# Seven products of quarter matrices for the up projection of a two-layer decoder step

## The reference

```
x = x + rmsnorm(mix, nm_post)
hf = jnp.einsum('btd,df->btf', rmsnorm(x, nf_pre), w_up)      # 1024 -> 4096
f = jnp.einsum('btf,fd->btd', jnp.square(jax.nn.relu(hf)), w_down)   # 4096 -> 1024
x = x + rmsnorm(f, nf_post)
```

## Time and profile before

| | |
|---|---|
| median of 3 runs | 2558.09 us (2558.03 to 2558.55) |
| profiled execution | 2556.82 us, of which the span of the trace is 2555.0 us |
| TensorE (PE) busy | 2509.7 us (98%) |
| VectorE (DVE) busy | 1397.3 us (55%) |
| ScalarE (ACT) busy | 795.3 us (31%) |
| GpSimd (POOL) busy | 963.2 us (38%) |
| mean granted TensorE clock | 0.998 |
| mean DMA rate | 73 GB/s |

### The profile page before, as it was taken

How to read it: one execution, slowest core, us unless ns; L and a number is a source line. 1 busy time by engine, 2 the same in 40 slices (tenths; PEclk the granted TensorE clock), 3 DMA queues, 4 the chain that set the end, 5 groups by cost and what they waited for, 6 DMA issues and landing times.

```text
span 2555.0 us, 45179 instructions
## 1 busy us (share of the span) xinstructions
PE 2509.7 (98%) x17828; PEld 2264.7 (89%) x17828; DVE 1397.3 (55%) x1966; ACT 795.3 (31%) x1281; POOL 963.2 (38%) x443
## 2 busy tenths in 40 slices
PE   8999999999999999999999999999999999999998
PEld 6996666988999999999989866669899999999998
DVE  5546666358346445643664566662684455345526
ACT  3125555234112111211441255551431112112214
POOL 2431000215664565455214300003065655664541
PEclk9999999999999999999999999999999999999999
DMA  6114332221111011010331153323211110111013
GB/s 229 44 38 127 90 88 83 110 83 60 67 50 47 35 52 63 22 61 33 135 118 42 40 135 89 87 67 118 85 51 66 50 66 16 66 49 57 25 42 144
DMA packets 99962, 187.12 MB, mean 73 GB/s; under 512 B 30704, under 2 KB 43184, under 8 KB 99824
## 3 DMA queue, kind: packets, MB, share of 16 engines
q1 hardware_dynamic: 97120, 176.83, 21.2%
q0 software_dynamic: 2560, 8.39, 1.2%
q10 hardware_dynamic: 144, 0.00, 0.0%
HBM read 158.85 MB, written 23.11 MB: 71 GB/s over the span
## 4 chain that ended last, share of the span: by engine, by line
PE 81%; issue 7%; DVE 5%; ACT 3%; POOLq 2%; POOL 1%; DVEq 1%; SPq 1%; DMA 0%; ACTq 0%
PE psum L1991 37%; PE psum L2487 21%; PE psum L2181 3%; PE psum L1976 3%; PE psum L2207 3%; PE psum L2193 2%; PE psum L2084 2%; PE psum L2228 2%; PE psum L2021 1%; ACT z L1010 1%; DVE stat L1569 1%; PE psum L2514 1%; PE psum L2264 1%; PE psum L2241 1%; PE psum L2239 1%
## 5 line engine op out<-in xcount | busy, mean ns | idle before, releaser
L1991 PE MATMUL psum<-hh,wh 128*128 128x352 f32 x2064 | 668.8, 324 | 0.8 <-DVE z L1419 0.8
L1991 PE MATMUL psum<-hh,wl 128*128 128x352 f32 x2064 | 662.8, 321 | 0.0
L1991 PE MATMUL psum<-hl,wh 128*128 128x352 f32 x2064 | 662.7, 321 | 0.0
L685 POOL TENSOR_TENSOR wh<-raw,ones 128x1024 fp32r<-128x1024 f32 x106 | 205.4, 1937 | 539.8 <-PE psum L1991 429.1
L2487 PE MATMUL psum<-hidh,wh 128*128 128x264 f32 x1344 | 384.6, 286 | 7.3 <-issue 4.1
L1991 PEld LDWEIGHTS psum<-hh,wh 128*128 128x128 f32 x2064 | 387.9, 188 | 2.6 <-issue 1.7
L1991 PEld LDWEIGHTS psum<-hl,wh 128*128 128x128 f32 x2064 | 388.5, 188 | 0.8
L1991 PEld LDWEIGHTS psum<-hh,wl 128*128 128x128 f32 x2064 | 387.5, 188 | 0.0
L2487 PE MATMUL psum<-hidl,wh 128*128 128x264 f32 x1344 | 383.7, 285 | 0.0
L2487 PE MATMUL psum<-hidh,wl 128*128 128x264 f32 x1344 | 382.8, 285 | 0.0
L1779 DVE TENSOR_TENSOR z<-psum,z 128x528 f32<-128x528 f32 x360 | 246.0, 702 | 129.4 <-PE psum L2487 129.4
(11 more groups left out here) (286 smaller groups left out, 4231.8 us busy)
## 6 DMA issues: line engine op xcount, KB each, us to landing
raw<-wst SPq DMA_DIRECT2D x104, 512.0 KB, 3.4
z<-cache_c SPq DMA_DIRECT2D x352, 64.0 KB, 1.9
x<-x_spill SPq DMA_DIRECT2D x4, 4224.0 KB, 14.5
t<-wst SPq DMA_DIRECT2D x56, 256.0 KB, 4.0
raw<-cache_c SPq DMA_DIRECT2D x160, 64.0 KB, 1.9
x_spill<-x SPq DMA_DIRECT2D x2, 4224.0 KB, 13.8
x_spill<-x SPq DMA_DIRECT2D x6, 1408.0 KB, 5.2
cn<-wst SPq DMA_DIRECT2D x28, 256.0 KB, 3.3
```

What stands on the lines that cost most here:

```text
L685: pool.tensor_tensor(wh[:, s, :], src, ones[:, 0:1].to_broadcast([P, TW]), ALU.mult)
L1991: ins = pe.matmul(bank3(u, g), w[:, s, o:o + P], m[:, k, cols(g)], start=(k == 0 and n == 0), stop=(k == kk - 1 and n == 2))
```

## The change

The up projection of blocks 1 to 7 is done like the down projection: seven products (`UPS`) of 512 x 512 weight quarters with 512 x 528 input quarters. I call them f0 to f6. A product is two units of 24 matmuls over 264 tokens.

**Input quarters.** Four sums of input quarters (T_1 to T_4) and the quarter B_22 are made once per layer: x is loaded again from DRAM in quarters (into space of `x2` and `hl`), ACT scales it with the gains (`gained`), DVE and POOL subtract, ACT and DVE make high and low parts (`high_t`, `low_t`), and SP stores both parts in DRAM (`keep`). The two right-hand places of `hh` and `hl` hold by turns what each product needs; from block 2 on ACT issues five loads per block (`load`), two DMAs of 1.08 MB each.

**Weights.** All eight quarters of a block are loaded as quarters by SP (`weights_of`); POOL makes the four sums for the up projection too (`sum_1` to `sum_4`), ACT all high parts and POOL all low parts (`low_one`).

**Out of PSUM.** ACT copies the first results (`copies`), DVE adds the others (`added`), and relu is now a separate DVE instruction from SBUF to SBUF for three of the four quarters (`relu_of`, `last_relu`).

The diff, cut to what matters. The products, each with its slot of weights (2 is `cw`), its input quarter, its PSUM bank set, and whether it starts it fresh:

```diff
+UPS = [(2, 0, 1, 1, True), (0, 0, 0, 0, True), (1, 1, 1, 0, False), (0, 0, 1, 1, False),
+       (1, 1, 0, 1, True), (0, 1, 1, 0, False), (1, 0, 1, 0, False)]
```

SP, once per layer, from block 0's down projection on (`splits(n)` waits for the n-th pair of weight parts, counted from g1's):

```diff
+                splits(1)
+                quarter_in(u21, up1, 1, 0, up_q)
+                sp.wait_ge(hl_new.sem, at.whole(hl_new, KD))
+                keep(B_22, 1, hq3_out)
...
+                sp.wait_ge(hq3_out.sem, at.value(hq3_out))
+                sp.dma_start(part_of(hl_raw, 0, 1), part_of(xs, 0, 0)).then_inc(xa_in.sem, 16)
+                sp.dma_start(part_of(x2, 0, 1), part_of(xs, 0, 1)).then_inc(xa_in.sem, 16)
+                sp.dma_start(part_of(hl_raw, 1, 1), part_of(xs, 1, 1)).then_inc(xb_in.sem, 16)
+                sp.dma_start(part_of(x2, 1, 1), part_of(xs, 1, 0)).then_inc(xb_in.sem, 16)
...
+                sp.wait_ge(t_lo.sem, at.value(t_lo, 1))
+                keep(T_1, 0, hq1_out)
+                splits(6)
+                quarter_in(u12, up1, 0, 1, up_a12)
+                sp.wait_ge(tr_pool.sem, at.value(tr_pool, 1))
+                sp.dma_start(flat(tq[1]), part_of(x2, 1, 1)).then_inc(hq3_out.sem, 16)
...
+                sp.wait_ge(t_lo.sem, at.value(t_lo, 2))
+                keep(T_2, 1, hq3_out)
...
+                def weights_of(tile, again, first):
+
+                    quarter_in(a22, tile + 4, 1, 1, dn_q, 0)
+                    quarter_in(a21, tile + 4, 1, 0, dn_q)
+                    quarter_in(a11, tile + 4, 0, 0, dn_a11, 2)
+                    quarter_in(a12, tile + 4, 0, 1, dn_a12, 3)
...
+                    quarter_in(u22, tile + 8, 1, 1, up_q, 5)
...
+                    quarter_in(u21, again, 1, 0, up_q, 6)
```

POOL, one block; the twelve low parts (one in each of `low_one` and `last_sum`) are for f2 to f6, g1 to g6 and the next f1, in this order:

```diff
+                def block_parts():
+
+                    low_one(1, u21)
+                    sum_3(u21, u22)
+                    sum_1(a21, a22, dn_q, up_full, 2)
+                    low_one(0, us4)
+                    low_one(1, u12)
+                    sum_2(a21, a11, dn_a11)
+                    low_one(0, u21)
+                    sum_4(s4, a12, a21, dn_a12)
+                    low_one(1, u22)
...
+                    low_one(0, s4)
+                    low_one(1, a11)
+                    sum_1(u21, u22, up_q, dn_full, PH)
                     low_one(0, a21)
+                    sum_3(a21, a22)
                     low_one(1, a21)
                     low_one(0, a22)
+                    next_ups()
                     low_one(1, a12)
...
+                    last_sum()
```

ACT in block 0, and then ACT in a later block from the end of f6 on (`weight(n)` makes the high part for POOL's n-th low part):

```diff
                     high_sum(3, two, 0, b12)
+                    gained(hl_raw, 0, 1, 0, xa_in)
+                    gained(x2, 0, 1, 0, xa_in)
                     high_sum(1, both, PH, b11)
                     at.step(s2_new)
                     act.wait_ge(s2_new.sem, at.value(s2_new))
                     high_down(0, 3, a21)
...
+                    high_down(0, 7, u11)
...
+                    high_t(1, 0, hq3_out, 48)
...
+                    load(T_1, 0, hq1_in, 14)
...
+                    weight(7, a11)
+                    square_of(b21)
+                    high_sum(3, both, 0, b12)
+                    high_sum(1, both, PH, b11)
+                    new_sum(s2_new)
+                    weight(8, a21)
+                    high_sum(2, both, 2 * PH, b12)
+                    new_sum(s3_new)
+                    weight(9, a21)
```

DVE, down projection of blocks 1 to 6 (`low(1, both, b11)` is for g4, and ACT's part of it is `high_sum(1, both, PH, b11)`):

```diff
+                        ups_of()
+                        less(b12, b22, b12, both).then_inc(h_sum.sem, 1)
+                        take(0, TURN)
+                        low(0, both, b11)
+                        dve.drain()
+                        low(3, both, b12)
+                        take(1, TURN)
+                        less(b11, b12, b11, both).then_inc(h_sum.sem, 1)
+                        squares_done(1)
+                        less(b12, b21, b12, both).then_inc(h_sum.sem, 1)
+                        take(2, TURN)
+                        low(1, both, b11)
+                        take(3, TURN)
+                        low(2, both, b12)
```

More of the change, by code:

```diff
@@ L181, in build @@
             pass
+        with nc.sbuf_tensor("hl_raw", [P, KD, TOK], F32) as hl_raw:
+            pass
         hl = sb("hl", [P, KD, TOK], F32R)
@@ L223, in build @@
         s4 = raw[:, 0, :]
+        u11, u12, u21, u22, us4 = a21, a12, raw[:, 0, :], raw[:, 1, :], a11
         b11, b12 = z[:, 8:10, 0:HB], z[:, 8:10, HB:TOK]
@@ L1238, in _ @@
+                first_half(False)
+                last_hid(0, 1, b12)
+                weight(5, u22)
+                for row, half, part in ((0, 0, b11), (1, 1, b22), (1, 0, b21)):
+                    square_of(part)
+                    last_hid(row, half, part)
+                at.step(up_full, UH)
                 act.wait_ge(fsq_free.sem, at.value(fsq_free))
@@ L1854, in block_of @@
-                    low(3)
-                    for m in range(UNITS_DOWN if not last else 4):
-                        if last and m == 2 and l < DEPTH - 1:
+                    for u in range(2):
+                        added(3, 1, 0, 1, u)
+                    relu_of(b12, 1)
+                    for u in range(2):
+                        added(4, 1, 0, 0, u)
+                    relu_of(b11, 0)
+                    added(5, 0, 1, 1, 0)
+                    low(0, 1, b12)
+                    added(5, 0, 1, 1, 1)
@@ L1857, in block_of @@
+                    relu_of(b22, 1)
+                    low(0, 0, b11)
+                    last_relu(0)
+                    last_relu(1)
+                    at.step(up_full, UH)
+                    at.step(up_act, 6)
+                    low(1, 1, b22)
+                    low(1, 0, b21)
+                    for m in range(4):
+                        if m == 2 and l < DEPTH - 1:
                             at.step(pre_in, 16)
```

606 lines of the change are left out of this document (433 added, 173 removed).

## The result

| | before | after |
|---|---|---|
| median of the runs on the same chip | 2558.32 us (2558.03 to 2560.24) | 2659.09 us (2654.28 to 2660.23) |
| ratio, 95% interval | | 1.0389 (1.0371 to 1.0407) |
| profiled execution, its span | 2556.82, 2555.0 us | 2659.99, 2658.2 us |
| forecast | | 2617 us, range 2558 to 2650 |

What follows compares the result with a forecast made beforehand. PE, busy in 98% of the span, was taken to bound the kernel. The terms gave 2556.8 - 64.8 + 50 + 34 + 40 = 2616.0, the median 1.3 above: 2617 us, 2.3% slower, range 2558 to 2650.

Steps and rivals of the forecast that it cites:

- matmuls saved, 7 blocks: Up projection, 7 blocks of 2 layers: seven products take 41.17 us in place of 45.80, 4.63 less each, -64.8 us.
- stops, block 0: Block 0's down projection: g3 waits for x, then g4's weight and g5 are held; 17 us a layer, +34 (23 to 38).
- stops, block 1, both projections: Block 1: f2, f3 and later operands wait for stores and loads, 20 us a layer; its down projection loses 4.2.
- stops, blocks 2 to 6: Down projection of later blocks: g2, g3, g4 late, 4.2 us a block; +50 us over blocks 1 to 6, both layers.
- block 7's end: End of block 7: costed at nothing, since 24 matmuls of down_first cover the last relu; without it some 2 us.
- the rival: Clock falls in the long stalls at f3 and g3: 4 stops, 5.88 us more each, 2640 us; chance 0.06.
- the trace has no such stop to tell: Clock: granted 1.00 in every stretch read, longest feed-forward stop 2.09 us, so no case of PE's clock falling when idle.
- The walk: A whole later block followed with DVE and POOL meetings: g2 1.3 late, g3 1.9, g4 1.0, sum 4.2 us.
- The least case: Down projection of a later block: g3 at least 1.06 late, 2.15 us in all the least a block can lose.
- The prediction's three parts: Block 0's down projection: g3 13.7 us late, g4's weight held 1.9, g5 held 2.6; together called 17 a layer.
- f2 and f3 together: Block 1's up projection: both products wait for stores and loads, 15 to 20 us late together, or 10.
- loads become the bound: Later blocks' up projection: 4.8 MB at 277 GB/s, T_4 2.8 us late in 12 blocks, 2651 us; chance 0.11.

Runs made afterwards that it cites:

- the first experiment: Changed kernel with the vector engine's difference for g3's quarter moved ahead of two takes and a low part in blocks 1 to 7; 2655.98 us, 1.0388.
- the run with SyncE's order: Changed kernel with only SyncE's block 0 transfers reordered: a22 and a21 ahead of T_2's store, B_22's store ahead of u21; 2627.47 us, 1.0272.
- the two runs with a stop made in the kernel before: Kernel before the change, ScalarE repeating the copy for g3's weight in the loop's blocks: three extra copies 2594.88 us, five 2627.55 us.
- the last version: Changed kernel with new SyncE, ScalarE, vector and GpSimd orders and T_1 loaded later, finally GpSimd's differences behind f5's and f6's low parts; 2557.29 us, 0.9987.

## Why the prediction was right in its side and wrong in its size

For the first layer, from the windows above (stops: length less busy PE, less what the kernel before had; clock: busy PE above full clock):

| us per layer | forecast | measured |
|---|---|---|
| matmuls saved, 7 blocks | -32.4 | -33 (86.9 - 82.2 = 4.7 each) |
| stops, block 0 | 17 | 14.6 - 3.0 = 11.6 |
| stops, block 1, both projections | 20 + 4.2 | 25.4 - 0.1 = 25.3 |
| stops, blocks 2 to 6 | 5 x 4.2 = 21 | 19.3 - 0.5 = 18.8 |
| block 7's end | 0 | 1.0 |
| PE at the lower clock | 0 | 5.1 + 8.7 + 8.8 = 22.6 |
| later start of g0 (2.8 of it not by the change, see below) | 0 | 617.99 - 611.48 = 6.5 |
| sum | 29.8 | 52.8 |

**The step that failed** is the clock: the sum had nothing for it, and it stood beside the sum as a rival only. Its mechanism was right, but it was given 0.06, four places and 5.88 us each, 23 in all. The loss is 22.6 us in the first layer and, by the same windows of the second, 16.2, so 39 in both: without it the changed kernel would stand at 2659 - 39 = 2620, beside a forecast of 2617. Both factors were off. A place cost less than a whole product at half clock: 13 to 27 of the 48 matmuls ran so, for 1.4 to 2.8 us. And there were 20 places and not 4: the rival was applied to stops over 10 us only, while stops from 1.9 us on brought it too, seven of them in the middle blocks. And "the trace has no such stop to tell" was not true: I had read the clock in the first layer, where the stop of 2.09 us had none behind it. The same place in the second layer of the kernel before has the answer:

```profile
1897.40 0.56 PE L2487 MATMUL psum<-hidh,wh 128*128 128x264 f32 x1 [2.06 <-issue]
```

```profile
1897.40:1904.80 7.40, 7.39 (x48) 7.40 (x49) 5.05 (x7) 2.44 (x3) 4.18 (x2) 0.77 0.00 1
```

A stop of 2.06 us, then a product of 7.4 at a clock of 0.77.

That all the rest comes to within 3 us is in part luck. The stops of the first layer are 56.7 us where 62.2 were forecast, and the later g0, which had no term, put 6.5 in their place.

**Waits of the middle blocks:** 4.2 a block forecast, 3.8 measured. The walk put 1.3, 1.9 and 1.0 before g2, g3 and g4; in block 3 and most others it was 0.3, 3.4 and 0. DVE's sum met not one but two instructions of GpSimd, so g3 took the whole delay and g4 none. The sum of a walk held where its places did not; for the clock the places mattered, since one stop of 3.4 costs a slow product and three of 1 to 1.7 do not (the first experiment). The least case, 2.15, came out as 2.2 when GpSimd's sums were out of the way.

**Block 0:** g3 forecast at 646.1, measured at 646.47, by the steps named: ACT's `gained` started at 635.58 behind the DMA, 0.8 later than forecast. Behind it PE stood 0.9 around g4 in place of 1.9, and 2.6 before g5 as forecast, from start to start. (The prediction's three parts, 13.7, 1.9 and 2.6, make 18.2 and not the 17 that it went on with.) The stops are only 11.6 where 17 were forecast because g3's time was set by the DMA and by ACT, whenever g0 began: 6.5 us of its lateness came out as a later g0. **Block 1:** f2 2.6 to 3 forecast, 4.2 measured; f2 and f3 together 15 to 20, measured 17.5; GpSimd's wait for the quarter behind T_2's store was the cause, as the run with SyncE's order showed with its 31.6 us.

**The later start of g0** had no term. 3.7 of its 6.5 us were in the units before g0: more of GpSimd's first `sum_1` now runs beside DVE's `low_h`, which took 10.02 us for five instructions in place of 6.24 in the kernel before. The sum waits for two quarters in place of four, and begins 3.1 us behind the start of `low_h` in place of 5.4. I costed the change from f0 on only. First the kernel before, then the changed one:

```profile
590.09 6.24 DVE L1380 SCALAR_TENSOR_TENSOR hl<-x,gn,hh 128x1056 fp32r<-128x1056 f32 x5
```

```profile
592.89 10.02 DVE L1663 SCALAR_TENSOR_TENSOR hl<-x,gn,hh 128x1056 fp32r<-128x1056 f32 x5
```

The other 2.8 us had built up before the feed-forward part, and are not the change's: the two runs with a stop made in the kernel before, whose code is the kernel before's up to there, begin the same five instructions at 592.89 and 593.01. So single executions differ by that much ahead of the part, and the first layer's loss by the change is some 50 us.

**Loads.** The rival "loads become the bound" is settled for the middle blocks: 182 GB/s at trips of 82.93 us, with no wait for them. In block 1 it was right in kind: f3's stop of 3.5 to 7.7 us in the first layer of the versions with SyncE's new order is ended by a load of B_22 (1.6 us where T_2's store was held back). ACT's share was also somewhat higher than taken: 0.53 and 0.65 us per DMA where I had 0.43.

**The middle blocks' cause** is shown to be order, not amount: in the last version the same 25 instructions of GpSimd take 61 us of 83, and the stops are gone. With GpSimd's order alone changed, g3's stop had fallen from 3.4 to 1.1. A trip fell by 87.82 - 82.93 = 4.9 us in the first layer and by 4.3 in the second. What remains is in blocks 0 and 1. Counted from the start of block 0's up projection, block 0 takes 9.5 us more than before the change in the first layer of the last version (670.05 - 592.85 for 655.95 - 588.26) and 8.2 in the second, and block 1 takes 11.3 and 11.6 more (98.37 and 98.66 for 87.03 and 87.05). That eats the gain of the matmuls. Whether it can be had back was not shown: splitting block 1's sum or taking its weights first left f3's stop, and holding back T_2's store moved it to f4.

## What to carry to other kernels

On a queue that makes small things with near due times (the low part of each weight) and large ones with far due times (the sum for the next stage), write down for each when it is wanted, and put the large ones in pieces behind the small ones; a place that looks free is only as free as the next due time behind it. When a stop of PE is moved or split, look at the clock behind it as well as at its length. And before you write that a trace has no case of something, look in every layer.

## What the runs showed of the hardware

I counted, over the feed-forward parts of all 18 traces, each stop of PE (distance of two matmuls' starts less 0.12 us) and whether the granted clock fell to 0.5 in the 48 matmuls behind it, or up to the next stop; there the matmuls follow each other at 0.22 us in place of 0.12:

| stop | stops | with half clock behind |
|---|---|---|
| 0.9 to 1.85 us | 316 | 0 |
| 1.85 to 2.2 us | 65 | 26 |
| 2.2 to 3.4 us | 82 | 60 |
| over 3.4 us | 129 | 125 |

At half clock PE runs at 1.2 GHz; the loss behind a stop was 1.4 to 2.8 us in the changed kernel. Behind the shorter stops the clock often fell only some matmuls into the product, up to 12, so a look at the first few misses it. The same stop, at the same place of the same loop, brings it or not, which is why the middle blocks of one kernel differ (86.93 to 88.87 us). The Trainium skill ("TensorE: Matmul & The Clock Gate", Part 1: The HAM clock gate) says that TensorE is throttled when idle and gets its clock back by activity, and that the point at which it comes back varies from run to run. The rows agree: behind the changed kernel's stops the full clock was back after 13 to 27 slow matmuls, and not always after as many at the same place. They also show the fall after stops of 1.9 us already.

The transfer engines carried 401 to 410 GB/s for stretches of 10 us in block 1 of two of the later versions, loads from DRAM and stores to it together, on two issuing queues. In the changed kernel ACT's reloads of 1056 KB took 5.1 us at least, 7.7 in the median and 15.3 at most (in block 1) to land, where 1056 KB would take 2.7 at that rate.
